# Hybrid decoder step on one core: memory rows turned before they are normed, prompt rows turned between value slabs, and two gate/up units without shared sums

## The reference

```python
def rmsnorm(x, w):
    y = x32 * lax.rsqrt(jnp.mean(x32 * x32, axis=-1, keepdims=True) + EPS)
    return (y * w.astype(F32)).astype(x.dtype)

def memory_kv(mem, p):                      # mem: 256 x 2048
    mn = rmsnorm(mem, p['norm_mem'])
    return mn @ p['xa_wk'], mn @ p['xa_wv'] # keys, values: 256 x 2048 each

def decoder_layer(x, ...):
    m, ... = mixer(rmsnorm(x, p['norm_mix_pre']), ...)   # begins with xn @ w_in
    x = x + rmsnorm(m, p['norm_mix_post'])
    x = x + rmsnorm(cross_attn(rmsnorm(x, p['norm_xa_pre']), mk, mv, p), p['norm_xa_post'])
    f = swiglu(rmsnorm(x, p['norm_ffn_pre']), p)         # (silu(x@gate) * (x@up)) @ down
    return x + rmsnorm(f, p['norm_ffn_post']), ...
```

## Time and profile before

| | |
|---|---|
| median of 3 runs | 3106.53 us (3104.11 to 3108.62) |
| the profiled execution: its own time | 3107.23 us |
| its span, first to last instruction | 3105.6 us |
| mean granted TensorE clock | 0.989 |
| PE busy | 3017.5 us (97%), 24088 matmuls |
| VectorE, ScalarE busy | 1885.3 us (61%), 1369.5 us (44%) |
| mean of one: slab high part (L1160), low part (L1914), square of a row tile (L1144) | 1.06 us, 1.23 us, 1.90 us |
| moved by DMA | 443.96 MB, mean 143 GB/s |

### The profile page before, as it was taken

The page is one execution under the profiler, slowest core; times in us unless marked ns, Lnnn a source line. Parts: engine busy times, 40 slices in busy tenths (PEclk is TensorE's granted clock), DMA queues, the critical chain, the costliest instruction groups (busy, mean ns, idle before and its releaser), DMA issues.

```text
span 3105.6 us, 60010 instructions
## 1 busy us (share of the span) xinstructions
PE 3017.5 (97%) x24088; PEld 2904.2 (94%) x24088; DVE 1885.3 (61%) x2718; ACT 1369.5 (44%) x2020; POOL 175.8 (6%) x220
## 2 busy tenths in 40 slices
PE   7999999999999999999996999999999999999999
PEld 5789999998889999987796999999999999999999
DVE  4644337454766477666369888888888883322323
ACT  5443444334365564334356555555555553321323
POOL 0000000001253000010000000000000001000010
PEclk9999999999999999999998999999999999999999
DMA  7563223332216557886664433334343335432323
GB/s 265 166 211 108 82 77 91 91 95 72 75 35 209 158 185 254 279 325 214 249 211 130 129 115 116 115 117 122 115 122 115 115 120 163 133 106 88 109 89 143
DMA packets 455077, 443.96 MB, mean 143 GB/s; under 512 B 22251, under 2 KB 417788, under 8 KB 446927
## 3 DMA queue, kind: packets, MB, share of 16 engines
q1 hardware_dynamic: 436746, 361.85, 37.7%
q0 software_dynamic: 12416, 69.55, 6.2%
q10 hardware_dynamic: 5776, 10.62, 1.0%
HBM read 408.26 MB, written 33.95 MB: 142 GB/s over the span
## 4 chain that ended last, share of the span: by engine, by line
PE 87%; DVE 7%; ACT 2%; DMA 2%; issue 1%; POOL 0%; ACTq 0%; DVEq 0%; SPq 0%; POOLq 0%
PE ps L2983 17%; PE ps L3590 16%; PE ps L3386 16%; PE ps L3558 9%; PE ps L3560 9%; PE ps L3559 9%; PE ps L2980 4%; DVE w_low L1914 1%; ACT w_high L1160 1%; DMA w_raw<-in_xa_wo 1%; PE ps L3477 1%; DMA q_wide<-q_mid 1%; PE ps L2932 1%; PE ps L3205 1%; PE ps L3016 0%
## 5 line engine op out<-in xcount | busy, mean ns | idle before, releaser
L1914 DVE TENSOR_TENSOR w_low<-w_raw,w_high 128x1024 fp32r<-128x1024 f32 x354 | 434.9, 1229 | 622.1 <-ACT w_high L1160 621.5
L3558 PE MATMUL ps<-set_high,w_hi 128*128 128x260 f32 x2464 | 700.1, 284 | 26.2 <-DVE set_low L2786 20.5
L3560 PE MATMUL ps<-set_high,w_lo 128*128 128x260 f32 x2464 | 699.2, 284 | 0.0
L3559 PE MATMUL ps<-set_low,w_hi 128*128 128x260 f32 x2464 | 699.0, 284 | 0.0
L1160 ACT ACTIVATE w_high<-w_raw 128x1024 fp32r<-128x1024 f32 x356 | 377.2, 1060 | 643.4 <-PE ps L3386 299.7
L3558 PEld LDWEIGHTS ps<-set_high,w_hi 128*128 128x128 f32 x2464 | 466.9, 189 | 30.0 <-DVE set_low L2786 23.7
L3560 PEld LDWEIGHTS ps<-set_high,w_lo 128*128 128x128 f32 x2464 | 467.8, 190 | 0.0
L3559 PEld LDWEIGHTS ps<-set_low,w_hi 128*128 128x128 f32 x2464 | 466.7, 189 | 0.0
L2983 PE MATMUL ps<-x_high,w_high 128*128 128x260 f32 x1568 | 318.6, 285 | 1.8 <-DVE w_low L1914 1.6
L2866 DVE TENSOR_TENSOR w_lo<-raw,w_hi 128x1024 fp32r<-128x1024 f32 x88 | 107.9, 1226 | 341.5 <-ACT w_hi L1801 341.5
L2983 PE MATMUL ps<-x_low,w_high 128*128 128x260 f32 x1568 | 314.4, 282 | 0.0
(11 more groups left out here) (536 smaller groups left out, 5584.6 us busy)
## 6 DMA issues: line engine op xcount, KB each, us to landing
w_raw<-in_w_in SPq DMA_DIRECT2D x96, 512.0 KB
raw<-in_ffn_w_up SPq DMA_DIRECT2D x176, 256.0 KB, 2.9
raw<-in_ffn_w_gate SPq DMA_DIRECT2D x176, 256.0 KB, 3.2
raw<-in_ffn_w_down SPq DMA_DIRECT2D x176, 256.0 KB, 3.0
w_raw<-in_w_out SPq DMA_DIRECT2D x64, 512.0 KB
w_raw<-in_xa_wq SPq DMA_DIRECT2D x64, 512.0 KB
w_raw<-in_xa_wo SPq DMA_DIRECT2D x64, 512.0 KB
w_raw<-in_xa_wk SPq DMA_DIRECT2D x32, 512.0 KB
```

The costliest lines, as they stand in the source:

```text
L1914: dve.tensor_tensor(w_low[:, slot], w_raw[:, (g.slab0 + jj) % RAW], w_high[:, slot].bitcast(F32), ALU.subtract).then_inc(sem("w_low_ready" ...
L3558: pe.matmul(ps[:, bank, 0:HALF], high, set_high[:, kp, x], start=kp == 0, stop=False)
L3559: pe.matmul(ps[:, bank, 0:HALF], high, set_low[:, kp, x], start=False, stop=False)
L3560: ins = pe.matmul(ps[:, bank, 0:HALF], low, set_high[:, kp, x], start=False, stop=kp == KP - 1)
```

## The change

1. The two halves of the memory rows are turned as they are loaded, in eight groups of two 128-column chunks through six banks (`mem_turn`). The norm weight comes as 16 rows of 128 that TensorE turns to a column (`mem_norm`), which is applied where ScalarE and VectorE take a group out of PSUM (`mem_turn_high`, `mem_turn_low`, two instructions of 256 columns each). The norm factor of a memory row is applied where a block of keys or values is taken (`take_kv`). The squares of the memory rows come after key slabs 3 and 4. Slab s of the first block waits only for group s. Five groups are split before the loop, the other three in it.
2. The prompt's norm weight and rows are loaded between key slabs 5 to 14, the sample rows before key slab 4, behind a wait for the first square. Small parameters and prompt rows are turned behind value slabs 0 and 2 to 18, one group behind each. Loops over the value slabs are written out.
3. Gate/up units 0 and 1 use eight plain products (192 matmuls), so slabs 0 to 7 need no sums and one instruction on each engine. Unit 0 waits for blocks 0 to 3 of a pair (`x_blocks`) instead of all seven.

The diff, cut:

```diff
-            for t in range(MT):
+            sp.dma_start(mem_norm_rows[0:NC, :], ...norm_mem...)
+            for t in range(MT):
                 sp.dma_start(mem_rows[:, t, :], ...)
-            sp.dma_start(norm_mem_row[:], i["norm_mem"].to_broadcast([P, D]))
...
-            sp.dma_start(norm_x_row[:], ...)
-            for t in range(TT):
-                sp.dma_start(x_rows[:, t, :], ...)
-            sp.wait_ge(sem("turned"), NC // 4)
+            sp.wait_ge(sem("turned"), mem_turns)
+            sp.wait_ge(sem("row_squares"), 1)
             sp.dma_start(xs_rows[0:B, :], ...)
...
                     for jj in range(RAW, g.blocks * g.slabs):
                         load(g, 0, jj)
+                        t = (jj - RAW) // 2
+                        if jj == RAW + 1:
+                            sp.dma_start(norm_x_row[:], ...)
+                        elif jj > RAW + 1 and jj % 2 and t - 1 < TT:
+                            sp.dma_start(x_rows[:, t - 1, :], ...)
```

```diff
+            def mem_turn_high(n):                       # ScalarE
+                for k in n:
+                    act.wait_ge(sem("turned"), k + 1)
+                    for q in range(2):
+                        ins = act.activation(mem_high[:, 2 * k + q], ps[:, mem_bank(k), q * M:(q + 1) * M], ACT.Copy,
+                                             scale=mem_norm[:, 2 * k + q:2 * k + q + 1])
+                    ins.then_inc(sem("turn_high"), 1)
+            mem_turn_high([0, 1])
             split_high(first_gemm, 0, 0)
             split_high(first_gemm, 0, 1)
+            mem_turn_high(range(2, MEM_AHEAD))          # MEM_AHEAD = 5
...
-                        ins = act.activation(kv_out[:, g.acc(j), m], ps[...], ACT.Copy)
+                        ins = act.activation(kv_out[:, g.acc(j), m], ps[...], ACT.Copy, scale=rstd_rows[:, m:m + 1])
...
+                    if k == 0:
+                        mem_turn_low(range(MEM_AHEAD, mem_turns))
+                    if k == MEM_ROOT_AT:                # 3
+                        row_rstd(0)
...
-            small_copies()
-            turn_low(range(mem_turns, len(turns)))
-            gemm(g_wv, nothing)
+            for n in range(g_wv.iters * g_wv.blocks * g_wv.slabs):
+                split_low(g_wv, 0, n + SPLIT)
+                if n == 0:
+                    small_copies()
+                if 0 <= n - X_TURN0 < X_TURNS:          # 2, 17
+                    turn_low([mem_turns + n - X_TURN0])
```

```diff
             def first_step(n):
-                slab_step(n, n % 4, tile=...)
+                dve.wait_ge(sem("w_high"), 2 * n + 2)
+                dve.tensor_tensor(w_lo[k][:, 0:8], raw[n % 4][...], w_hi[k][:, 0:8].bitcast(F32), ALU.subtract)
...
-            slab_step(-1, 3, low=False, loaded=32)
...
-            combine(0)
+            plain_combine(0)
...
-            up_unit(1, 0, None)
+            scale(0)
+            first_step(7)
+            slab_step(7, 3, low=False)
+            hidden(0, 0, None)
+            for k in range(3):
+                slab_step(8 + k, k)
+            plain_combine(1)
...
-            products(0, FIRST_TILES, 0, first=True)
+            plain_unit(0, FIRST_TILES, first=True)
...
+            plain_unit(1, range(4))
+            pe.wait_ge(sem("x_set"), KP)
```

More of the change, by code:

```diff
@@ L1163, in turn_high @@
                 for k in n:
-                    t, c, per, rows, to = turns[k]
+                    t, c, per, rows, to = turns[k - mem_turns]
                     act.wait_ge(sem("turned"), k + 1)
@@ L3538, in squares_summed, with plain_unit @@
                     pe.matmul(ps[:, 7, GN[1]:SEQ], ones[:], square_of(c), start=c == 0, stop=c == NC - 1).then_inc(sem("xa_summed"), 1)
-            def products(n0, tiles, n, first=False):
+            def plain_unit(n, tiles, first=False):
+                for s, k in enumerate(tiles):
+                    pe.wait_ge(sem("w_low"), 4 * n + s + 1)
+                    for j, g, (bank, terms) in itertools.product(range(2 if first else 1), range(2), PLAIN_PRODUCTS):
+                        if first and (g, bank) == (0, 0):
+                            squares_summed(2 * s + j - 1)
+                            pe.wait_ge(sem("x_blocks"), 2 * s + j + 1)
+                        if s == 0 and not first:
+                            if (g, bank) == (0, 0):
+                                pe.wait_ge(sem("first_copied"), n)
+                            elif bank == 1:
+                                pe.wait_ge(sem("combined"), 4 * n - (3 if g == 0 else 0))
+                        for half in ((j,) if first else range(2)):
+                            kp = 2 * s + half
+                            for q, (which, x) in enumerate(terms):
+                                w = 4 * half + 2 * (which == "odd") + 1 - g
+                                high, low = w_hi[k][:, w], w_lo[k][:, w]
+                                out = ps[:, 3 * g + bank, 0:HALF]
+                                pe.matmul(out, high, set_high[:, kp, x], start=kp == 0 and q == 0, stop=False)
+                                pe.matmul(out, high, set_low[:, kp, x], start=False, stop=False)
+                                ins = pe.matmul(out, low, set_high[:, kp, x], start=False, stop=kp == KP - 1 and q == len(terms) - 1)
+                        if s == 3 and (j or not first) and 3 * g + bank < 5:
+                            ins.then_inc(sem("done"), 2 if 3 * g + bank == 4 else 1)
+                    ins.then_inc(sem("w_used"), 1)
@@ L3542, in products @@
+            def products(n0, tiles, n):
                 for s, k in enumerate(tiles):
                     pe.wait_ge(sem("w_low"), n0 + (s + 1))
-                    for j, (bank, (w, x)) in itertools.product(range(2 if first else 1), enumerate(PRODUCTS)):
-                        if first and bank == 0:
-                            squares_summed(2 * s + j - 1)
-                            pe.wait_ge(sem("x_set"), 2 * s + j + 1)
-                        if s == 0 and not first:
+                    for bank, (w, x) in enumerate(PRODUCTS):
+                        if s == 0:
@@ L3554, in products @@
                                 pe.wait_ge(sem("combined"), 4 * n - 5 + min(bank, 5))
-                        for half in ((j,) if first else range(2)):
+                        for half in range(2):
                             kp = 2 * s + half
```

178 lines of the change are left out of this document (118 added, 60 removed).

## The result

The changed kernel takes 3089.12 us (median of 3 runs, 3087.22 to 3089.60) against 3106.53: ratio 0.9945, 95% interval 0.9931 to 0.9959. Forecast: 3087, range 3080 to 3094. The profiled execution's own time is 3089.12 us, its span 3087.5 us at a mean clock of 0.993, so it is compared with 3107.23 and 3105.6 us.

A forecast was written before the change was run, and what follows sets the result against it. TensorE, busy for 97% of the span, was taken as the bound. Gains of 8.0 + 3.7 + 8.0 = 19.7 us off 3107.2 gave 3087.5, with the median 0.7 lower, say 3087; range 3080 to 3094.

The forecast's parts named there:

- part 3: Gate/up units 0 and 1: plain products and earlier starts bring unit 2 nearer; 8.0 us gained (6 to 10).
- part 1: The start and the key slabs: memory rows turned as loaded; 8.0 us gained (4 to 10).
- groups 0 and 1 are high at 12.1: Start: the first two memory-row groups have their high parts at 12.1 us, low parts at 13.1.
- Slab 4: Key slab 4, issued at 25.8 behind the first square's wait, starts at 32.1 instead of 40.83: 8.7 us gained.
- The half clock that follows is the same in both: Keys behind slab 4's stall: 0.67 of full clock before and after the change, so no difference.
- made up in the next one; nothing: Keys: prompt-row squares on ScalarE every second slab, 1.06 + 2.1 us against 2.74 a slab, cost nothing.
- 0.7 us for contention: Keys: prompt rows sharing DMA engines with key slabs lose 0.7 us (0 to 4).
- rival 1: Key slabs 8 to 15 starve behind prompt rows: 8 us, 7.3 more than counted, 3094 in all; chance 0.12.
- Part 2: Keys to values: transposes spread between value slabs cost 11.9 us instead of 15.6; 3.7 us gained (1.2 to 6).
- If VectorE's chain had cover, 3 us better still: Unit 1's end: with cover for VectorE's chain after the reciprocal, PE would set the end at 1716.3.
- 0.7 us for the clock: Unit 2's start: shorter PE waits save 0.7 of the 1.9 us lost to slow clock before.
- Rival 5: Units 0 and 1: TensorE stays at half clock because unit 0 is fed in bursts; 11 us slower, 3118; chance 0.02.

The follow-up runs named there:

- e_kv_table: The changed kernel with ScalarE's table load ahead of its first wait, and its stored-keys/values waits moved into the token gemm's first padded eviction: 3084.58 us, ratio 0.9934.
- e_slab4: The changed kernel with the sample rows' load and the waits ahead of it moved from before key slab 4 to behind key slab 15: 3081.97 us, ratio 0.9929.
- only_plain: The kernel before the change, with only the plain products of gate/up units 0 and 1 added: 3097.20 us, ratio 0.9968.
- e_small: The changed kernel with the 43 small transposes in four pieces behind value slabs 0 to 3, prompt groups two slabs later: 3087.20 us, ratio 0.9940.
- e_block: The changed kernel with small parameters and prompt rows turned in one block between keys and values again: 3091.94 us, ratio 0.9949.
- e_recip: The changed kernel with VectorE's reciprocal of the norm placed ahead of slab 6's rest instead of behind it: 3086.58 us, ratio 0.9931.
- e_combine: The changed kernel with unit 1's evictions on ScalarE and VectorE placed ahead of slab 10 instead of behind it: 3083.90 us, ratio 0.9925.
- best: The changed kernel with late sample rows, early table load, moved store waits, small transposes in four pieces and unit 1's evictions ahead of slab 10: 3074.85 us, ratio 0.9894.

## Why the prediction was right, step by step

The time lies in the range and part 3 came as worked out. Parts 1 and 2 were put 4.4 us too high, most of it in part 1; that the profiled pair shows 18.1 of the 19.7 us is in part luck.

- **First key matmul, forecast 14.5, measured 16.05.** Landing (10.0), transposes and evictions came as worked out. The step that failed is "groups 0 and 1 are high at 12.1": it left out the table load. In before the load came at 5.83 us, behind the first half of the rows, and was done before the second half landed (9.64); in after the first activation waits for a turned group, and the load behind that wait is on the path. e_kv_table shows its whole price, 1.3 us. I had allowed 0.7 us for a table load at the square; no run shows that figure: in after no load stands at the square, and each load in the traces takes 1.28 us.
- **Slab 4, forecast 32.1, measured 33.10.** The wait behind the square was named and its landing of 4.0 us was 4.10. The late first key matmul is the difference. e_slab4 shows that the stall was a matter of order alone.
- **"The half clock that follows is the same in both"** was wrong: behind slab 4's stall 11 matmuls were 0.43 us apart in after and 7 in before. In before that was chance, too: its repeat had 8, only_plain, the same program there, had none, and every profile with slab 4's longer stall had 10 to 13. The squares, "made up in the next one; nothing", were not quite that: slab 18 waits 0.8 us where before's longest wait there was 0.4, and the chain that ended last runs to it through the sample rows' square, the root and the first block's eviction on ScalarE (67.4 to 74.0 us). So the keys gained 5.8 us in this pair and 4.6 by the means, not 8.0. The 0.7 us for contention and rival 1 found nothing to support them: no slab from 8 to 15 waited.
- **Part 2, 3.7 us.** The price of a transpose was right: a group of four stretches the slab's 2.74 us to 3.21, 0.117 each where I had 0.12. Half pace wherever transposes stand is out: the clock is 1.00 from 130 to 134 us. Missing was what the small ones do to the clock: 10 matmuls in 3 us behind them (e_small shows the cause; e_block has it too, on transposes). Net 2.1 us from the end of the keys to the last value matmul in this pair, 2.8 by the means. Behind it 0.7 us were lost in this pair to the store of values. PE had no gap there in before, but one of 0.6 us in its repeat; the seven profiles with spread values and without e_kv_table's edit have 0.2 to 0.7 us.
- **Part 3, 8.0 us.** Unit 1 begins 56.0 us behind the last `xa_wo` matmul (forecast 57, before 63.3), the waits are 1.48 and 1.20 us (forecast 1.5 and 1.3), the second product is 8.3 us nearer (forecast 7.3). The reason given for the chain was partly wrong: it runs on VectorE, but from slab 7, not from the reciprocal (e_recip). "If VectorE's chain had cover, 3 us better still" was right: 3.1 (e_combine). The 0.7 us for the clock has no true value; it is 0 in after, and its repeat's last column is 2.6 shorter. Rival 5 was argued against with a wrong reading: in before the clock was not full from the second half slab of unit 0 on, but at 0.50 again at 1663.3 to 1666.3 us and at 0.51 at 1690.8 to 1693.8. In after it is at 1.00 from 1648 to 1651 and from 1674 to 1677 us.
- **The sum.** By the means of the profiles, parts 1 and 2 gave 4.6 and 2.8 us, 7.3 together, instead of 11.7; part 3 gave 8.3 instead of 8.0, and 1.5 more in the last column (2.4 in five of the eight profiles that have part 3 and its waits). That makes 17 us, as the medians say (17.4), where 19.7 were forecast: the errors cancelled only in small part, and the range took in the rest. In the profiled pair another 3 us came between 325 and 1635 us, with the pair and not with the change.

Not settled: why PE waits 18.6 us for `set_low` in unit 0 after the change as it did 20.5 before; no run touched it.

## What to carry to other kernels

When work leaves the front of an engine's program, ask what was hidden behind its wait: here a table load of 1.28 us and, in a queue, a wait that stood ahead of every later slab; they cost 1.3 and 7 us. An engine that is busy without a break can still be the wrong suspect for its amount of work: the order in which it served the others was worth 3.1 us, and moving its largest instruction was worth nothing. Before explaining a difference in code that two kernels share, take the same kernel's profile twice.

## What the runs showed of the hardware

A run of 43 transposes of 24, 8 or 112 rows, PE busy all the time by the profile, was followed in after by nine matmuls at half clock (granted 0.50, 0.43 us apart instead of 0.23), two of them in part; behind the same transposes in four pieces (e_small, best) they are 0.22 to 0.24 us apart but for the first behind a piece (0.33 or 0.34). Full-size transposes alone did run at a clock of 1.00 (e_block, 128 to 133 us), after 0.50 at 122 to 125 us. Behind the same idle times of 1.5 and 1.2 us the clock was 0.50, 0.62 and 0.62 for 4.5 us in three of eight profiles (after, only_plain, e_block) and 1.00 in five, which makes 1.6 to 2.7 us at that place (unit 2). Over 1400 us of unchanged code 13 profiles differ by up to 5.9 us; in them 10 to 21 us of it were at half clock, and PE's idle time was 27.8 to 31.8 us.
